# A hybrid decoder step on one Trainium2 core: prompt attention unrolled, values stationary in column halves, row-sum reciprocals turned

## The reference, cut to what matters

```python
MLA_HEADS, QK_NOPE, QK_ROPE, V_HEAD, SEQ = 16, 64, 32, 64, 1024
k_nope = einsum('bkc,chd->bkhd', ckv, w_uk)          # ckv: 256 latent rows
v      = einsum('bkc,chd->bkhd', ckv, w_uv)
sc = einsum('bqhd,bkhd->bhqk', qn, k_nope) + einsum('bqhr,bkr->bhqk', qp, kpe)
sc = where(k_pos <= q_pos, sc * ATT_SCALE, -inf)
p  = softmax(sc, axis=-1)
o  = einsum('bhqk,bkhd->bqhd', p, v)                 # then x = x + gate * (o @ w_o)
```

## Time and profile before

| | before |
|---|---|
| median of 3 runs | 3555.71 us |
| span of the profiled execution | 3551.2 us |
| its own time beside the span | not given apart |
| TensorE (PE) busy | 3206.8 us, 90% |
| VectorE (DVE) busy | 1585.6 us, 45% |
| POOL busy | 1057.2 us, 30% |
| ScalarE (ACT) busy | 656.0 us, 18% |
| mean granted TensorE clock | 0.935 |

### The profile page before, as it was taken

One profiled execution on the slowest core, in us unless ns is written; L12 is line 12 of the kernel. 1 busy time (PEld: TensorE's weight loads), 2 busy tenths in 40 slices (PEclk: granted clock), 3 DMA queues, 4 the chain that ended last, 5 costly groups with the idle time before them and its releaser, 6 DMA issues.

```text
span 3551.2 us, 46136 instructions
## 1 busy us (share of the span) xinstructions
PE 3206.8 (90%) x18048; PEld 2762.0 (78%) x18048; DVE 1585.6 (45%) x2414; ACT 656.0 (18%) x976; POOL 1057.2 (30%) x424
## 2 busy tenths in 40 slices
PE   5699899987999999999668999999899899999997
PEld 2668687775888889888657777777646799999997
DVE  2423233234545444445555554545311655554554
ACT  3221111122000000000333222323122300100001
POOL 2213121232434433344321111110002335444443
PEclk9889899899999999999889989899887999999998
DMA  4223233221211211111100000000221111111111
GB/s 163 67 77 104 62 99 89 74 61 68 72 65 70 80 63 59 59 65 59 50 15 33 10 20 15 20 15 22 56 66 48 50 42 53 42 47 46 48 47 56
DMA packets 86436, 200.53 MB, mean 56 GB/s; under 512 B 25018, under 2 KB 43834, under 8 KB 85470
## 3 DMA queue, kind: packets, MB, share of 16 engines
q1 hardware_dynamic: 85970, 197.45, 17.7%
q10 hardware_dynamic: 336, 1.25, 0.1%
HBM read 188.07 MB, written 10.61 MB: 56 GB/s over the span
## 4 chain that ended last, share of the span: by engine, by line
PE 84%; DVE 7%; ACT 4%; DMA 3%; issue 2%; SPq 0%; POOL 0%; DVEq 0%; POOLq 0%; ACTq 0%
PE ps L523 59%; PE ps L491 5%; PE ps L1404 4%; PE ps L1432 3%; DMA ada_raw<-in_ada_units 3%; PE ps L1416 2%; PE ps L1655 1%; PE ps L504 1%; PE ps L1027 1%; PE ps L1698 1%; PE ps L1050 1%; PE ps L1392 1%; PE ps L1019 1%; DVE norm_buf_f L642 1%; DVE q_rot_samples L1532 0%
## 5 line engine op out<-in xcount | busy, mean ns | idle before, releaser
L461 POOL TENSOR_TENSOR w_hi<-w_raw,ones 128x1024 fp32r<-128x1024 f32 (+1 forms) x195 | 473.2, 2427 | 2133.3 <-PE ps L523 1996.6
L464 POOL TENSOR_TENSOR w_lo<-w_raw,w_hi 128x1024 fp32r<-128x1024 f32 (+1 forms) x195 | 514.3, 2637 | 15.3
L523 PE MATMUL ps<-hn_head_f,w_hi 128*128 128x344 f32 x2112 | 453.4, 323 | 38.1 <-DVE hn_rest_f L657 33.9
L523 PE MATMUL ps<-hn_rest_f,w_hi 128*128 128x344 f32 x2112 | 448.4, 321 | 0.0
L523 PE MATMUL ps<-hn_head_f,w_lo 128*128 128x344 f32 x2112 | 448.1, 321 | 0.0
L523 PEld LDWEIGHTS ps<-hn_head_f,w_hi 128*128 128x128 f32 x2112 | 356.5, 189 | 41.9 <-issue 31.9
L523 PEld LDWEIGHTS ps<-hn_rest_f,w_hi 128*128 128x128 f32 x2112 | 357.5, 189 | 0.0
L523 PEld LDWEIGHTS ps<-hn_head_f,w_lo 128*128 128x128 f32 x2112 | 354.6, 189 | 0.0
L560 DVE SCALAR_TENSOR_TENSOR x<-ps,mod,x 128x688 f32<-128x688 f32 x208 | 194.3, 934 | 310.3 <-PE ps L523 310.3
L491 PE MATMUL ps<-ada_raw,silu_c 128*9 128x512 f32 x448 | 223.9, 634 | 59.8 <-DMA ada_raw<-in_ada_units 59.2
L523 PE MATMUL ps<-h_head,w_hi 128*128 128x344 f32 x1056 | 226.6, 323 | 7.5 <-DVE h_rest L776 7.5
(11 more groups left out here) (351 smaller groups left out, 4758.6 us busy)
## 6 DMA issues: line engine op xcount, KB each, us to landing
w_raw<-in_w_units SPq DMA_DIRECT2D x187, 512.0 KB, 3.4
ada_raw<-in_ada_units SPq DMA_DIRECT2D x120, 512.0 KB, 3.6
pages_ckv<-in_cache_ckv SPq DMA_DIRECT2D x64, 128.0 KB, 2.0
x<-in_x SPq DMA_DIRECT2D x8, 516.0 KB, 7.0
row_bcast<-row_scratch SPq DMA_DIRECT2D x4, 1032.0 KB, 6.0
out_y<-y_tiles SPq DMA_DIRECT2D x8, 516.0 KB, 3.0
state_s<-in_state_C SPq DMA_DIRECT2D x4, 1024.0 KB, 8.1
out_C_sample<-state_s SPq DMA_DIRECT2D x4, 1024.0 KB, 10.3
```

Of the source, the lines that this page charges most:

```text
L461: pool.tensor_tensor(hi[s][:, 0:n, :], raw[u % 2][:, 0:n, :], ones[:, :].unsqueeze(1).to_broadcast([P, n, P]), ALU.mult).then_inc(w_head, 1)
L464: pool.tensor_tensor(lo[s][:, 0:n, :], raw[u % 2][:, 0:n, :], hi[s][:, 0:n, :].bitcast(F32), ALU.subtract).then_inc(w_split, 1)
L523: mm = nc.tensor.matmul(out(c), w, v[:, a:b], start=(first and p_ == 0), stop=(last and p_ == 2))
```

## The change

The loop is unrolled over 8 pairs p, with fills and weight units numbered by functions instead of loop registers. The tiles of a pair are now ordered by blocks of 256 queries: n = 4 m + 2 e + t is head e, query block 2 m + t. A unit u = n // 2 is two neighbouring query blocks of one head, turned together into chunks: chunk j holds the key blocks 2 j and 2 j + 1 for both query blocks, 4 blocks of 128 (3 in the last chunk). Chunks and the turned inverses share banks 6 and 7 alternately; ten buffers hold the copied chunks (six in `p_turned`, four in `ada_raw`) in place of four, `p_exp` has four in place of two. For the values, `v_tokens` of one head (128x64) is stationary and 256 queries stream (128 for the last key block); head 0 writes partitions 0 to 63 of the result, head 1 partitions 64 to 127, and the heads alternate. The result so has features on partitions. Its scale is made by 16 reciprocals per pair that write 128x64 from one broadcast row sum, turned on PE in two blocks for each m (`inv`), copied by ScalarE, multiplied by VectorE, and split into head and rest 256 columns at a time. The last values of a pair are issued behind the next pair's queries and keys, and the projection behind these. Core of the diff:

```diff
+    CHUNKS = []
+    for u_ in range(8):
+        if u_ >= 3 and u_ % 2:
+            CHUNKS.append(("inv", (u_ - 3) // 2, 0))
+        CHUNKS += [("p", u_, j) for j in range(u_ // 2 + 1)]
+    CHUNKS.append(("inv", 3, 0))
+    NCH = len(CHUNKS)
...
+    def chunk_take(pe, p, c):
+        at = CHUNKS.index(c)
+        if at >= 2:
+            q, before = p, CHUNKS[at - 2]
+        elif p:
+            q, before = p - 1, CHUNKS[at - 2 + NCH]
+        else:
+            return
+        if before[0] == "p":
+            pe.wait_ge(pt_copied[at % 2], copies_before(q, before) + 1)
+        else:
+            pe.wait_ge(inv_copied, 4 * q + before[1] + 1)
...
+        def scores(p, n):
+            e, qt, T = n % 4 // 2, n // 4 * 2 + n % 2, score_fill(p, n)
+            take(T)
+            w = (qt + 1) * P
+            for c in range(0, w, 512):
+                mm = pe.matmul(flat(T, min(512, w - c), c),
+                               N["q"][0:96, e, qt * P:(qt + 1) * P],
+                               N["k"][0:96, e, c:min(w, c + 512)], start=True, stop=True)
+            mm.then_inc(full, 1)
+        def turn(p, u):
+            m = u // 2
+            ev(pe, score_fill(p, 2 * u + 1))
+            for j in range(m + 1):
+                chunk_take(pe, p, ("p", u, j))
+                side, _ = chunk(("p", u, j))
+                at = 0
+                for kb in (2 * j, 2 * j + 1):
+                    for t_ in range(2):
+                        if kb <= 2 * m + t_:
+                            mm = pe.transpose(ps[:, 6 + side, at:at + P],
+                                              N["pex"][:, (2 * u + t_) % 4, kb * P:(kb + 1) * P],
+                                              ident[:, :])
+                            at += P
+                mm.then_inc(pt_full[side], 1)
+        def values(p, m, kbs):
+            o = ps[:, 2 + 3 * (m % 2), 16:16 + 256]
+            if kbs[0] == 0:
+                if 4 * p + m >= 2:
+                    pe.wait_ge(o_free, 4 * p + m - 1)
+                if m == 0:
+                    ev(pe, v_fill(p))
+            for kb in kbs:
+                for e in range(2):
+                    c = ("p", 2 * m + e, kb // 2)
+                    if kb % 2 == 0 or kb == kbs[0]:
+                        pe.wait_ge(pt_copied[chunk(c)[0]], copies_before(p, c) + 1)
+                    a = P if kb == 2 * m + 1 else 0
+                    mm = pe.matmul(o[64 * e:64 * e + 64, a:256],
+                                   N["v"][:, kb, e * 64:(e + 1) * 64],
+                                   N["pt"][ring_at(c)][:, 256 * (kb % 2):256 * (kb % 2) + 256 - a],
+                                   start=(kb == 0), stop=(kb == 2 * m + 1))
+            if kbs[-1] == 2 * m + 1:
+                mm.then_inc(o_full, 1)
+                c = ("inv", m, 0)
+                chunk_take(pe, p, c)
+                side, _ = chunk(c)
+                pe.wait_ge(ri_ready, 4 * p + m + 1)
+                for t_ in range(2):
+                    mm = pe.transpose(ps[:, 6 + side, t_ * P:(t_ + 1) * P], N["ri"][:, m % 2, t_, :], ident[:, :])
+                mm.then_inc(pt_full[side], 1)
...
+        for p in range(PAIRS):
+            queries_keys(p)
+            if p:
+                values(p - 1, 3, range(8))
+            if p and p % 2 == 0:
+                out(p // 2 - 1)
+            values_of_tokens(p)
+            ev(pe, pair_fill(p, TK))
+            pe.wait_ge(q_ready, 1 + p)
+            for n in range(2):
+                scores(p, n)
+            for u in range(1, 9):
+                if u < 8:
+                    scores(p, 2 * u)
+                if u >= 3:
+                    m = (u - 3) // 2
+                    values(p, m, range(m + 1) if u % 2 else range(m + 1, 2 * m + 2))
+                if u < 8:
+                    scores(p, 2 * u + 1)
+                turn(p, u - 1)
+        values(PAIRS - 1, 3, range(8))
+        out(3)
...
+    def copy_chunks(eng, p, u, side, N):
+        for j in range(u // 2 + 1):
+            c = ("p", u, j)
+            if chunk(c)[0] == side:
+                chunk_full(eng, p, c)
+                k = 20 * p + P_CHUNKS.index(c) - 10
+                if k >= 0:
+                    eng.wait_ge(o_full, 4 * (k // 20) + P_CHUNKS[k % 20][1] // 2 + 1)
+                w = 384 if j == u // 2 else 512
+                dst, src = N["pt"][ring_at(c)][:, 0:w], ps[:, 6 + side, 0:w]
+                ins = eng.tensor_copy(dst, src) if side else eng.activation(dst, src, ACT.Copy)
+                ins.then_inc(pt_copied[side], 1)
...
+        def inverse_rows(p, m):
+            c = ("inv", m, 0)
+            side, _ = chunk(c)
+            chunk_full(act, p, c)
+            if 4 * p + m >= 2:
+                act.wait_ge(at_ready, 4 * p + m - 1)
+            act.activation(N["att"][:, m % 2, :], ps[:, 6 + side, 0:256], ACT.Copy).then_inc(inv_copied, 1)
+        def head_of_out(p, m):
+            act.wait_ge(o_free, 4 * p + m + 1)
+            act.activation(N["ath"][:, p % 2, 256 * m:256 * m + 256], N["att"][:, m % 2, :], ACT.Copy)\
+               .then_inc(at_head, 1)
+        def exps(p, n):
+            qt, T = n // 4 * 2 + n % 2, score_fill(p, n)
+            w = (qt + 1) * P
+            act.wait_ge(nm_ready, 16 * p + n + 1)
+            if 16 * p + n >= 4:
+                pq, u = divmod((16 * p + n - 4) // 2, 8)
+                chunk_full(act, pq, ("p", u, u // 2))
+            act.activation(N["pex"][:, n % 4, 0:w], flat(T, w), ACT.Exp,
+                           bias=N["nm"][:, n % 4:n % 4 + 1], accum_out=N["rs"][:, n % 8:n % 8 + 1])\
+               .then_inc(free[T % 2], 1)
...
+            if p:
+                inverse_rows(p - 1, 3)
+                head_of_out(p - 1, 3)
+            exps(p, 0)
+            exps(p, 1)
+            for u in range(1, 9):
+                for n in (2 * u, 2 * u + 1):
+                    if n < 16:
+                        exps(p, n)
+                if u >= 3 and u % 2 == 0:
+                    inverse_rows(p, u // 2 - 2)
+                copy_chunks(act, p, u - 1, 0, N)
+                if u >= 3 and u % 2 == 0:
+                    head_of_out(p, u // 2 - 2)
+        inverse_rows(PAIRS - 1, 3)
+        head_of_out(PAIRS - 1, 3)
...
+        def inverses(p, m):
+            for n in range(4 * m, 4 * m + 4):
+                e = n % 4 // 2
+                ev(dve, score_fill(p, n))
+                ins = dve.reciprocal(N["ri"][:, m % 2, n % 2, 64 * e:64 * e + 64],
+                                     N["rs"][:, n % 8:n % 8 + 1].to_broadcast([P, 64]))
+                if n % 4 == 3:
+                    ins.then_inc(ri_ready, 1)
+                else:
+                    S.done(ins)
+        def out_scaled(p, m):
+            dve.wait_ge(inv_copied, 4 * p + m + 1)
+            dve.wait_ge(o_full, 4 * p + m + 1)
+            dve.tensor_tensor(N["att"][:, m % 2, :], ps[:, 2 + 3 * (m % 2), 16:16 + 256],
+                              N["att"][:, m % 2, :], ALU.mult).then_inc(o_free, 1)
+        def out_rest(p, m):
+            dve.wait_ge(at_head, 4 * p + m + 1)
+            dve.tensor_tensor(N["atl"][:, p % 2, 256 * m:256 * m + 256], N["att"][:, m % 2, :],
+                              N["ath"][:, p % 2, 256 * m:256 * m + 256].bitcast(F32),
+                              ALU.subtract).then_inc(at_ready, 1)
...
+        for p in range(PAIRS):
+            rotate(p)
+            if p:
+                out_scaled(p - 1, 3)
+                out_rest(p - 1, 3)
+            if p and p % 2 == 0:
+                add_out(p // 2 - 1)
+            T = v_fill(p)
+            fl(dve, T)
+            dve.tensor_copy(N["v"][:, :, :].rearrange("p j c -> p (j c)"), flat(T, SEQ))\
+               .then_inc(free[T % 2], 1)
+            row_max(p, 0)
+            row_max(p, 1)
+            for u in range(1, 9):
+                for n in (2 * u, 2 * u + 1):
                     if n < 16:
-                        copy_group(dve, n, 1, i, pp, N)
-                    if n:
-                        out(n - 1)
-                dve.wait_ge(at_head, 1 + pp + 2 * i)
-                dve.tensor_tensor(N["atl"][:, pp, :], flat(T(20), SEQ), N["ath"][:, pp, :].bitcast(F32),
-                                  ALU.subtract).then_inc(free[T(20) % 2], 1)
-            for m in range(KT):
-                T42 = T_PAIR + 42 + m
-                fl(dve, T42, i, TPP)
-                dve.scalar_tensor_tensor(x[:, m, 0:SEQ], flat(T42, SEQ), mod[:, MODL + GT1 + m, 0:1],
-                                         x[:, m, 0:SEQ], ALU.mult, ALU.add).then_inc(free[T42 % 2], 1)
+                        row_max(p, n)
+                if u % 2 == 0:
+                    inverses(p, u // 2 - 1)
+                    if u >= 3:
+                        out_scaled(p, u // 2 - 2)
+                copy_chunks(dve, p, u - 1, 1, N)
+                if u >= 3 and u % 2 == 0:
+                    out_rest(p, u // 2 - 2)
+        out_scaled(PAIRS - 1, 3)
+        out_rest(PAIRS - 1, 3)
```

(67 more changed lines are left out.)

292 lines of the change are left out of this document (99 added, 193 removed).

## The result

The changed kernel takes **3598.2 us** in the median of 4 runs (3595.3 to 3605.0), the kernel before 3558.0 beside it; the ratio is 1.0111, 95% interval 1.0082 to 1.0139. So it is slower by about 40 us, where the forecast had 124: the sign was right and the time lies in the range, but the change was forecast three times too large. The time is near the rival whose halves overlap (3625 us, or 3598 with no extra low clock).

What follows compares the result with a forecast made beforehand. The prediction took the prompt attention as bound by TensorE work plus waits. To the 3551.2 us span it added 98 for waits and 27 for low clock, 3676, put at 3680 us; range 3590 to 3735.

Steps and rivals of the forecast that it cites:

- the rival whose halves overlap: Value products of two heads run together, waits unchanged: 55 us less, 3625 us, or 3598 without extra low clock; chance 0.34.
- Values: Value products on TensorE: the heads' halves follow each other, 15.4 us a pair as before; 7.7 if fully overlapped.
- the forecast's own case: Prompt attention with the value halves one after another, more waits and low clock: around 3680 us; chance 0.42.
- Waits: TensorE waits in the prompt attention: 42.2 us a period against 17.6, +98 us in all.
- the write-out: Iterations u=1 to u=8 of a pair, listed as TensorE work and wait: 32.7 us work, 20.1 us wait.
- Clock: Low clock behind idles of 2.5 us or more: two stretches of 1.7 us a pair, +27 us (ends 0 and +70).
- a clock of 1.00 after idles of 3 us: Sign of a wrong forecast: TensorE's granted clock stays full after long idles, where low stretches were expected.
- Change of width: TensorE drain when values alternate with full-width products: no row priced it, so it entered no term.
- Order: Copies queued behind two exps or maxima: third chunk's turn waits about 2.8 us; 20.1 us of waits a pair.
- Stagger: Last values moved behind the next pair's queries and keys: hides the rotation's wait of 1.50 us.
- The faster one: Copies in the prompt attention arrive in time: 3521 us, or 3466 with overlapping halves; chance 0.13.
- clock collapse: TensorE runs half of a pair's 32.7 us of work at the low level: +90 us, 3770 us; chance 0.05.

Runs made afterwards that it cites:

- x5_one_half: Changed kernel with both heads' value products sent to one column half, so none overlap (result wrong, timing only): 3656.5 us.
- x2_copyfirst: Changed kernel with ScalarE copying the turned inverses and its first chunk ahead of the second exponential: 3563.6 us.
- y3_dvefirst: y2_compact with VectorE also copying its first chunk ahead of the second row maximum in units of three and four chunks: 3498.5 us.
- y2_compact: Changed kernel with ScalarE's copies early, reciprocals behind VectorE's copies, and four reciprocals made one of 128x4 plus one broadcast copy: 3506.4 us.

## Why the prediction was right in sign and too large

**Values, the step that failed.** "I take 15.4", one half after the other, was wrong by 7.7 us a pair. x5_one_half is the forecast's own case and takes 3656.5; 58 of the 82 us between 3680 and 3598 are this term. The rival had its price right, 55. That its second figure, 3598, is the measured time is luck: it stands for no extra low clock, and 30 us of it came; waits written out too long made up for them. My argument against it, that the second record of a head must follow its first, holds for one head and does not stop the other's. Where no row shows a case and a rule speaks for it, nearest rows of another case (full-width products) were a poor bound.

**Waits, right in place and too long.** 24 us are left. Two pairs of x5_one_half, from the first score to the next pair's queries:

```profile
2366.58:2424.35 57.77, 45.48 (x176) 26.27 (x176) 31.96 (x65) 18.98 (x45) 4.69 (x2) 0.85 0.03 10
2285.16:2341.07 55.91, 43.70 (x176) 25.38 (x176) 31.95 (x65) 18.98 (x45) 5.94 (x4) 0.88 0.09 29
```

In the first the iterations u=1 to u=8, by the starts of their first records, take 5.3, 3.6, 5.1, 6.6, 7.0, 10.1, 14.2 and 5.9 us, 57.8 in all. The low level takes 8.5 of these (1.4, 1.8, 0.2, 0, 0, 0.5, 3.7 and 0.9), where the sum has 4.9 of old and 3.4 of new, 8.3. What is left is 49.3, and the write-out had 4.3, 2.5, 6.4, 6.7, 7.1, 10.4, 10.2 and 5.2, 52.8: 3.5 too much, 28 us in eight pairs. 1.5 of it is u=3 and 0.8 u=6, both with the reciprocals at 2.4 us for 1.78; 1.1 is u=1 and u=2. TensorE is idle for 12.3 us in this pair, where I had waits of 20.1; the other part of the difference is busy time beyond my 32.7 us of work, such as the tails of the records, which my pitches leave to the waits. Waits do not hide the low clock: the second pair is idle for the same 12.2 us, loses 6.8 us to the low level in place of 8.5, and is 1.9 us shorter.

**Clock.** +30 us against +27, but in part by luck. The low stretches stand behind the idles inside a pair, as forecast; each costs 3.4 us and not 1.7, and their number changes from pair to pair, where I had two in each: from the first score to the next pair's queries the pairs lose 3.4 to 11.8 us, where those of before lose 4.9 in the mean. I had named a clock of 1.00 after idles of 3 us as a sign of being wrong; the pair with idles of 2.25 to 2.72 us and a clock of 0.99 comes close to it. My upper end of +70 was also added up wrongly: four stretches of 1.7 us in each of eight pairs are 54.

**Change of width.** The prediction put the drain at nothing, as no row priced it. The rows of the changed kernel do. PE before the last values of a pair:

```profile
2388.61 0.63 PE L563 MATMUL ps<-ck_rest,w_hi 128*128 128x512 f32 x2
2389.08 0.63 PE L563 MATMUL ps<-ck_head,w_lo 128*128 128x512 f32 x2
2389.64 0.43 PE L1523 MATMUL ps<-p_turned,v_tokens 128*64 128x256 f32 x1
```

Two records take 0.47 us before others of full width and 0.56 before the values. Likewise a score record of 384 columns is followed after 0.32 us by another score and after 0.42 by a value, and the first score behind the values starts 0.31 us after the last 256 columns, not 0.215. Each change costs 0.09 us, 112 of them in the stage some 10 us (an estimate). It fits that x5_one_half, whose work the forecast put equal to the old, keeps TensorE busy for 591 us of its stage without what the low level takes, where the kernel before has 573. Whether it is a drain or the wait for a weight load, no run tells.

**Order.** Right in place: third chunk, inverse copy and VectorE's copy are the rows that grew, and x2_copyfirst takes 35 us out by moving two copies. The longest is 2.7 us, as forecast, but the idle time before turns that a copy ends is 9 us a pair (39.7 + 20.0 + 13.3 in eight pairs) and not some 20, and the turns' weight loads are idle for 111.5 us against 76.0, not twice that. A period (a quarter of the stage) came to 178.1 us; in x5_one_half, which has the forecast's values, to 192.6, where I had 198.

**Stagger.** Priced at one hidden wait of 1.5 us a pair; it is worth 28 to 42 us in all. That did not harm the sum, which took no waits at a pair's end.

**The other rivals.** The faster one named its condition, a third chunk that hardly waits, with 3466 us when the halves overlap. y3_dvefirst meets it at 3498.5. What it lacks is neither waits nor clock: its stage is idle for 34.3 us, where the rival has 8.8 a period, 35, and loses 42.5 us to the low level, where the rival has 47. So the 32 us are busy time beyond the sum of the pitches, of which the changes of width are a part; no run takes the others apart. There was no clock collapse: 0.89 in the stage.

## What to carry to other kernels

When two tiles are worked off as one unit, look at each in-order queue for the short copy that now stands behind two long operations: moving three such pieces ahead or behind turned +1.1% into -0.7%, and a lighter reciprocal and one more early copy into -1.7%. An edit that brings nothing can be worth 30 us once the later of two waits is gone, so try them together too. Before you believe an experiment that swaps an order, see in its trace that the order is swapped, and take out what the clock gave or took: the same edit cost 15, 31 and 17 us in three versions, and 35, 28 and 32 without the clock.

## What the hardware showed unexpectedly

- Products in different column halves keep no common order: a record of the second half started with three of the first, earlier in the program, still to come. Two fp32 streams of 256 columns with 64 stationary ones each start every 0.215 us, both at once.
- Behind idles of 2.24 and 2.72 us the granted clock was 0.51 over seven us in one pair, and behind idles of 2.25, 2.72 and 2.50 us it was 0.99 in the pair before; fewer waits did not always give a higher clock (y3_dvefirst lost 42.5 us to it with fewer waits than y2_compact, which lost 33.8). Why, no run here tells.
- Going from records of full width to those of a column half, or back, cost TensorE 0.09 us each time.
- A reciprocal of 128x64 takes 0.445 us in a row of four, one of 128x4 0.17, a broadcast copy of 128x256 0.29.
